# A hybrid attention block on one core: the first attention block prepared during the last weight tile, and group B's last product packed into one bank

## The reference

```python
proj = x @ W_in                       # one projection, its columns shared out
# group A: 8 query heads, one key/value head
dots  = qi . ki                       # 4 index heads
score = sum_h w_h * relu(dots)        # per query and key, chunk-causal
idx   = top_k(score, 256)             # per query
ya    = softmax(qa . ka[idx] / 8 - slope * |distance|) @ va[idx]
# group B: 8 query heads, 2 key/value heads, window of 128 keys, a sink per head
yb    = softmax([qb . kb / 8 - slope * |distance|, sink])[:-1] @ vb
y     = concat(ya * silu(ga), yb * silu(gb)) @ W_out
out   = layer_norm(2 ** 0.25 * x + y) * g + b
```

## Time and profile before

| | before |
|---|---|
| median of 3 runs | 1454.12 us (1453.76 to 1454.82) |
| profiled execution | 1462.23 us, span 1460.4 us |
| PE busy | 1359.3 us (93%) |
| DVE busy | 1130.6 us (77%) |
| ACT busy | 896.8 us (61%) |
| POOL busy | 629.6 us (43%) |
| last product ends, first scan starts | 555.7 us, 572.1 us |
| output projection starts | 1275.8 us |

### The profile page before, as it was taken

The page is one execution under the profiler, slowest core; times in us unless marked ns, Lnnn a source line. Parts: engine busy times, 40 slices in busy tenths (PEclk is TensorE's granted clock), DMA queues, the critical chain, the costliest instruction groups (busy, mean ns, idle before and its releaser), DMA issues. The chain is left out here.

```text
span 1460.4 us, 18810 instructions
## 1 busy us (share of the span) xinstructions
PE 1359.3 (93%) x6006; PEld 993.5 (68%) x6052; DVE 1130.6 (77%) x2215; ACT 896.8 (61%) x1687; POOL 629.6 (43%) x726
## 2 busy tenths in 40 slices
PE   7999999899999995798999799999999799999997
PEld 5888887698888874565655456655555565588886
DVE  3486879864899887778889999889898967257675
ACT  3395885873498736777775488885678676700010
POOL 2421332633422336466544256534336577423332
PEclk9999999999999996699999999999999899999999
DMA  7412232325232328233433132402011143134442
GB/s 241 127 60 80 87 105 80 117 91 154 73 109 94 101 90 174 66 89 87 113 92 88 45 83 56 104 21 64 27 28 26 39 133 118 44 122 146 144 148 83
DMA packets 106548, 136.85 MB, mean 94 GB/s; under 512 B 6643, under 2 KB 83383, under 8 KB 106191
## 3 DMA queue, kind: packets, MB, share of 16 engines
q1 hardware_dynamic: 93296, 93.23, 23.4%
q10 hardware_dynamic: 9504, 31.66, 5.5%
q0 software_dynamic: 3648, 10.76, 2.5%
HBM read 92.20 MB, written 42.34 MB: 92 GB/s over the span
## 5 line engine op out<-in xcount | busy, mean ns | idle before, releaser
L1644 DVE TENSOR_SCALAR_CACHE_REDUCE above<-dist,trial 128x512 bf16<-128x512 int32 (+13 forms) x224 | 345.9, 1544 | 28.9 <-POOL trial L1002 23.9
L1179 ACT ACTIVATE above<-dist,trial 128x384 bf16<-128x384 int32 (+13 forms) x224 | 280.8, 1254 | 60.8 <-DVE trial L1617 24.3
L1356 PE MATMUL psum<-x_hi,w_hi 128*128 128x512 f32 x640 | 251.8, 393 | 16.0 <-DVE x_lo L1693 10.6
L1356 PE MATMUL psum<-x_lo,w_hi 128*128 128x512 f32 x640 | 250.8, 392 | 0.0
L1356 PE MATMUL psum<-x_hi,w_lo 128*128 128x512 f32 x640 | 250.5, 391 | 0.0
L1290 ACT ACTIVATE prob<-psum 128x512 f32<-128x512 f32 x272 | 159.8, 593 | 115.8 <-PE psum L1506 54.6
L1748 DVE CUSTOM_DVE_ANT_0 junk<-psum,mask 128x512 bf16<-128x512 f32 (+3 forms) x320 | 184.4, 605 | 26.7 <-PE psum L1430 16.1
L1506 PE MATMUL psum<-prob,vw 128*65 128x512 f32 x376 | 184.8, 597 | 0.1
L1493 PE MATMUL psum<-qa_mix,ka_mix 128*128 128x512 f32 x272 | 162.4, 597 | 5.5 <-DMA qa_ext<-minus_max 3.7
L1430 PE MATMUL psum<-ka_ext,qa_ext 128*128 128x512 f32 (+3 forms) x320 | 134.1, 467 | 27.4 <-ACT ka_mix L1129 12.3
L941 POOL CAST w_hi<-raw 128x1024 fp32r<-128x1024 f32 x40 | 49.7, 1243 | 253.1 <-PE psum L1356 248.8
(11 more groups left out here) (161 smaller groups left out, 2906.8 us busy)
## 6 DMA issues: line engine op xcount, KB each, us to landing
raw<-w_tiles SPq DMA_DIRECT2D x40, 512.0 KB, 3.7
proj<-staged ACTq DMA_DIRECT2D x40, 512.0 KB, 3.3
qb_raw<-proj SPq DMA_DIRECT2D x32, 256.0 KB, 4.0
qa_raw<-proj SPq DMA_DIRECT2D x32, 256.0 KB, 4.5
yt_raw<-y_t SPq DMA_DIRECT2D x16, 512.0 KB, 5.1
x_row<-x_res SPq DMA_DIRECT2D x16, 512.0 KB, 3.9
out<-z ACTq DMA_DIRECT2D x16, 512.0 KB, 2.6
x_raw<-xT SPq DMA_DIRECT2D x12, 512.0 KB, 4.2
```

What stands on the lines that cost most here:

```text
L1179: nc.scalar.activation(above[:, 0, 0:n], src, ACT.Sign, scale=-1.0, bias=u, accum_out=count[:, 0:1]).then_inc(sign_counted, 1)
L1356: last = pe.matmul(psum[:, 2 * u + m, :], wt[:, u, k, :], xt[:, k, 512 * m:512 * m + 512], start=(k == 0 and q == 0), stop=(k == KT - 1 an ...
L1644: v.tensor_scalar(above[:, 1, 0:n], src, u, None, ALU.is_ge, ALU.add, accum_out=count[:, 1:2]).then_inc(own_counted, 1)
```

## The change

Three things are edited, and a fourth follows from them.

1. **Earlier conditions at the seam.** The products of the last tile now count up `x_used` for each k slice. `last_tile(k)` waits for one slice instead of the whole tile, and the loads, POOL's DMAs and the first rounding of queries use slices 0 to 6 by what each overwrites; three late tensors are placed elsewhere for that (`qa_raw`, `junk` and `y_a`). Group A's keys are read into `values_hi` and `values_lo` instead of `relu`, during the second half of the projection, and are rounded there; `split_values` waits for them. The first scan waits for the evacuation of the last tile but one.
2. **Constants on POOL.** The memsets of `setup_pieces` move from DVE to POOL (`fill`), each behind the slice that frees its place.
3. **Group B's last product.** Each of the four matmuls of `mix_b` has 64 weight columns, writes 64 rows, and all go to bank 2; `gate_b` is one instruction of 128 rows in place of two of 64.
4. **A new order.** All 165 numbers of `PREFER` differ, and POOL's decisions cost 0.53 instead of 0.45 in the plan, so nearly every engine's order differs from the first microseconds on.

```diff
-PREFER = {'above': -36689.1, 'band0': -163507.6, 'band1': 5353.3,
+PREFER = {'above': -229823.5, 'band0': -129160.3, 'band1': -191364.3,
...
-    add("SP", 0.7, "load_keys_a", needs=[sums[-1], ("store", 1, 2)])
+    last = lambda k: ("product", 1, N_TILES - 1, k)
+    add("SP", 1.4, "load_keys_a", needs=[("store", 1, 2)])
...
-    add("DVE", 1.8, "setup_dve", needs=[end])
+    for i in range(2):
+        add("POOL", 0.35 if i else 2.2, "fill", i, needs=[end if i else last(5), ("fill", i - 1)])
...
-        keys_a_raw = flat(relu)
+        keys_a_raw = [values_hi[:, :, :].bitcast(F32).rearrange("p b n -> p (b n)")[:, 0:HALF],
+                      values_lo[:, :, :].bitcast(F32).rearrange("p b n -> p (b n)")]
+
+        def last_tile(k):
+
+            return (x_used, KT + k) if k < KT - 1 else (tile_mm, 2 * N_TILES)
...
             def load_keys_a():
                 sp.wait_ge(stored[0], 16 * (N_TILES // 2 + 2))
-                sp.wait_ge(summed, 4 * chunks_before(NPAIR - 2))
...
             def extra_rows():
-                pool.wait_ge(tile_mm, 2 * N_TILES)
+                pool.wait_ge(*last_tile(4))
...
+            def fill(top):
+
+                pieces = [(2, mask[:, 0, 0:P], 0.0), (2, mask[:, 1, 0:2 * P], 0.0), (2, mask[0:HD, 0, HD:P], -BIG),
+                          (2, mask[0:HD, 1, P + HD:2 * P], -BIG), (2, lb[:, :, 0:HD], 0.0), (5, vs[0:HD, 0, :], 0.0),
+                          (KT - 1, row_top[:, :], 0.0)]
...
             def round_keys_a(i):
                 ks = slice(HALF * i, HALF * (i + 1))
-                act.wait_ge(keys_in, 32)
+                act.wait_ge(keys_in, 64)
+                act.wait_ge(x_lo_ok, 2 * KT + 2)
...
-                    pe.wait_ge(tile_out, 2 * N_TILES)
+                    pe.wait_ge(tile_out, 2 * N_TILES - 1)
...
+                        rows = slice(HD * g, HD * g + HD)
-                        last = pe.matmul(psum[:, 2 + g, 2 * P * c:2 * P * c + 2 * P], keys, ptb[:, g, 2 * P * c:2 * P * c + 2 * P],
+                        last = pe.matmul(psum[rows, 2, 2 * P * c:2 * P * c + 2 * P], keys[:, rows], ptb[:, g, 2 * P * c:2 * P * c + 2 * P],
                                          start=True, stop=True)
...
-                for g in range(2):
-                    rows = slice(HD * g, HD * g + HD)
-                    last = v.tensor_tensor(yt_b[rows, :, :].rearrange("p h (c q) -> p c h q", c=2),
-                                           psum[rows, 2 + g, :].rearrange("p (c h q) -> p c h q", c=2, h=4),
-                                           gate_b[rows, :, :].rearrange("p h (c q) -> p c h q", c=2), ALU.mult)
-                last.then_inc(b_gated, 1)
+                v.tensor_tensor(yt_b[:, :, :].rearrange("p h (c q) -> p c h q", c=2),
+                                psum[:, 2, :].rearrange("p (c h q) -> p c h q", c=2, h=4),
+                                gate_b[:, :, :].rearrange("p h (c q) -> p c h q", c=2), ALU.mult).then_inc(b_gated, 1)
```

More of the change, by code:

```diff
@@ L215, in dots_of @@
                 add("DVE", 0.33 + n / 960, "search", p, i, needs=[start, ("decide_own", p, i - 1)])
-                add("POOL", 0.45, "decide_own", p, i, needs=[("search", p, i)])
+                add("POOL", 0.53, "decide_own", p, i, needs=[("search", p, i)])
                 add("ACT", 0.49 + (n - P) * 0.00083, "sign", p, i, needs=[start, ("decide_sign", p, i - 1)])
-                add("POOL", 0.45, "decide_sign", p, i, needs=[("sign", p, i)])
+                add("POOL", 0.53, "decide_sign", p, i, needs=[("sign", p, i)])
             else:
@@ L337, in whole_plan @@
         add("POOL", 3.6, "split_qb", b, needs=[("round_qb", b)])
-        add("SP", 0.7, "load_qa", b, needs=[("split_qa", b - 1)] + ([end] if first else []))
+        add("SP", 0.7, "load_qa", b, needs=[("split_qa", b - 1)] + ([last(0), ("store", 1, 7)] if first else []))
         if b >= 2:
             add("SP", 0.4, "load_mask", b, needs=[("store_masks", b // 2), last_values(b - 2)])
-        add("ACT", 1.75, "round_qa", b, needs=[("load_qa", b)] + ([last_values(b - 2)] if b >= 2 else [end]))
+        add("ACT", 1.75, "round_qa", b, needs=[("load_qa", b)] + ([last_values(b - 2)] if b >= 2 else [last(KT - 2)]))
         add("POOL", 2.0 if b else 0.9, "positions", b, needs=[("extra_rows",)] + ([last_values(b - 2)] if b >= 2 else []))
@@ L348, in whole_plan @@
             add("DVE", 1.45, "bias_b", b, g,
-                needs=[("window", b, g), ("turn_b", b - 1), ("load_bias",), ("setup_dve",), ("put_sink", b), ("exp_b", b - 1, H - 1)])
+                needs=[("window", b, g), ("turn_b", b - 1), ("load_bias",), ("fill", 0), ("put_sink", b), ("exp_b", b - 1, H - 1)])
         for h in range(H):
@@ L360, in whole_plan @@
                 needs=[("round_qa", b), ("positions", b), ("leave_max", b - 1), scan_list[-2], ("scan", *scan_list[-1][1:]),
-                       ("extra_rows",), ("load_power",), ("round_keys_a", 1), ("evacuate", 1, N_TILES - 1)])
+                       ("extra_rows",), ("load_power",), ("round_keys_a", 1), ("evacuate", 1, N_TILES - 2)])
             scan_list.append(("scan_max", *scan))
-            add("DVE", 0.16 + w * 0.00104, "scan_max", *scan, needs=[("scan", *scan), ("load_mask", b), ("setup_dve",), scan_list[-2], *stores])
+            add("DVE", 0.16 + w * 0.00104, "scan_max", *scan, needs=[("scan", *scan), ("load_mask", b), ("fill", 1), scan_list[-2], stores[1], end])
         if b >= 4:
@@ L372, in whole_plan @@
         add("PE", 1.8, "mix_b", b, needs=[("copy_b", b), ("shift_values",)], holds="banks2", until=("gate_b", b))
-        add("DVE", 1.35, "gate_b", b, needs=[("mix_b", b), ("load_gate_b", b), ("store_b", b - 1)])
+        add("DVE", 0.71, "gate_b", b, needs=[("mix_b", b), ("load_gate_b", b), ("store_b", b - 1)])
         add("POOL", 1.0, "store_b", b, needs=[("gate_b", b)])
@@ L1359, in product @@
                     last.then_inc(tile_mm, 1)
[L1360 removed]
+                elif t == N_TILES - 1:
                     last.then_inc(x_used, 1)
@@ L1741, in scan_max @@
                 if scan == 0:
-                    for i in range(2):
-                        dve.wait_ge(stored[i], 16 * N_TILES)
+                    dve.wait_ge(stored[0], 16 * N_TILES)
+                    dve.wait_ge(tile_mm, 2 * N_TILES)
+                    dve.wait_ge(filled, FILLS)
                 dve.wait_ge(a_scan, scan + 1)
```

85 lines of the change are left out of this document (40 added, 45 removed).

## The result

The changed kernel takes 1461.0 us (median of 4 runs, 1459.35 to 1462.96) against 1453.94 for the kernel before in the same measurement: ratio 1.0049, interval 1.0032 to 1.0067. It is 0.5% slower, about 7 us. Its profiled execution took 1460.82 us, span 1459.0. The time lies inside the predicted range of 1430 to 1462, near its top, but the sign is wrong: the forecast was 1445. The range held it because it had been drawn over the rivals too; alone the forecast spanned 1437 to 1451.

The account below looks back on a forecast made before the run. PE and DVE were taken to bound the kernel in turns, with DVE's chain of pairs behind. Seam +5.5, start +2, gates -6.9 and pair 6 -9 gave -8.4 us: 1445 us forecast, chance 0.36, range 1430 to 1462.

Parts of the forecast that it names:

- The seam's PE side: End of projection: products end 9.1 us earlier, first scan 6 to 8 us behind; 9 to 12 us gained for PE alone.
- The lateness of pair 4: Second projection half: ten dots pieces later, so pair 5's first sum comes 13.6 us later, at 539.3.
- 15 us idle for the same work: DVE from pair 5's first sum to block 1's leave_max: 15 us idle instead of about 20, winning 5 back.
- +5.5: DVE's chain at the seam, at block 1's leave_max: 13.6 - 5 - 1.1 - 2, so 5.5 us later.
- Pair 6, -9: Around 825 us: PE's waits for y_a and block 8's leave_max go, 9 us gained, bounds 0 and 13.
- The rest of the order, 0 with 6 either way: Pieces moved throughout the kernel: no row gives a sign, so 0 with 6 us either way.
- Gates -6.9: gate_b as one instruction saves DVE 0.69 us in ten blocks where DVE leads: -6.9 us, bounds 0 and 11.
- PE's term 0: mix_b on PE: same columns and place in the chain, so no change; bounds 3.5 us either way.
- That rival: mix_b: the two key groups' matmuls run side by side, about 6 us more gained, 1439 us; chance 0.03.
- The start, +2: First projection half: PE waits 2 us for low parts before norm pieces; bounds +1.5 and +3.6.
- the late pairs decide: Sums of pair 4: the 13.6 us pass whole, y_a's stall returns; +5.6 us, 1460 us; chance 0.26.
- the forecast's own signs of being wrong: Pair 5's first sum not late, block 1's leave_max well before 600, or PE idling over 10 us up to pair 6's sortable end.

Follow-up runs that it names:

- e0: The kernel before, unchanged, run again for a second profile; 1455.93 us.
- e2: The changed kernel with group B's product as before (128 weight columns, two banks, two gate instructions), in the new order; ratio 1.0121 to the kernel before.
- e1: The kernel before with only group B's product changed, every engine's order untouched; 1451.34 us, ratio 0.9974.
- e7: e1 with the last scans and leave_max of block 8 ahead of pair 6's sortable, and scans and logits ahead of block 7's columns_a; 1457.68 us.
- e3: All edits of the changed kernel, PE's and DVE's order as in the kernel before, group A's keys rounded earlier, ahead of a relu; 1456.78 us.
- e4: The changed kernel with the order of the kernel before from the first search step of pair 6 on; 1461.5 us, ratio 1.0036.
- e5: e3 with group A's keys rounded during sortable of pair 4, so all edits in the old order; 1443.47 us, ratio 0.9915 to the kernel before.
- e9: The changed kernel's new order up to the last product, from there the order of the kernel before; 1455.28 us, ratio 1.0010.
- e12: e5 with all pieces of pair 4, dots, relu and sums of pair 5, and the keys' copies 13.7 us later; 1462.53 us.
- e15: e5 without block 0's early conditions: of the seam only the keys stay early; 1450.3 us, ratio 0.9962 to the kernel before.
- e10: e5 with only dots, relu and sums of pairs 4 and 5 (and the keys' copies behind them) 13.7 us later; 1468.32 us, ratio 1.0105.
- e11: As e10 with half the delay, 6.85 us; 1462.1 us, ratio 1.0056 to the kernel before.
- e13: All edits; new order only up to the end of tile 1 of the second half, then the order of the kernel before; 1455.77 us.
- e16: All edits; new order only up to the last product of the first half, then the order of the kernel before; 1452.63 us.
- e6: The changed kernel with mix_b packed into one bank but gate_b as two instructions of 64 rows; 1470.37 us, ratio 1.0095.
- e14: e1 with both key groups' matmuls writing rows 0 to 63, group 1's into bank 3; ratio 1.0005 to the kernel before.
- e17: The changed kernel with the order of the kernel before up to the last product of the first half; 1462.41 us, ratio 1.0044.

## Why the prediction was wrong, step by step

**The seam's PE side** held: the last product ended at 545.3 and the first scan started at 550.1 (said: about 549, and 6 to 8 us behind; it was 4.8), and the wait for the keys is gone.

**The lateness of pair 4** held too: 13.6 us were predicted at the first sum of pair 5 (539.3; the 541 in the list of signs does not follow from the sum), and 13.0 were measured against e0.

**"I give the changed kernel 15 us idle for the same work"** is the step that failed first. The term was +5.5 (bounds -4.5 and +10.5), read at `leave_max` of block 1. DVE's chain does not pass there any more. Measured with group B's change taken out (e2 against e0), the kernel is 13.3 us late at Q6 (841.9 against 828.6), where seam and pair 6 together had -3.5. Busy time from S5 to Q6 (the third pair of numbers is DVE), e0 first, then e2:

```profile
526.00:828.56 302.56, 253.44 (x1087) 168.51 (x1104) 255.89 (x591) 208.91 (x383) 149.03 (x215) 0.91 0.41 98
539.60:841.85 302.25, 257.20 (x1098) 167.32 (x1113) 266.51 (x617) 208.30 (x398) 145.63 (x223) 0.90 0.39 95
```

Over this longer stretch DVE's idle time fell from 46.7 to 35.7 us, more than the 5 I gave. What failed is "for the same work": DVE's busy time there rose by 10.6 us, where I had taken 3.1 off, and so nothing of the lateness came back. Of the 10.6 us, 8.0 are the second line of the sums, which got slower (below; 25.3 us in e2 from 520 to 600, 17.4 in e0), and the rest is not split here; three gate instructions more stand ahead of Q6. In the changed kernel the sums of pair 5 took 46.0 us (539.0 to 585.0) instead of 29.6, with scans and biases between them.

**Pair 6, -9,** failed outright: "What follows, 850 to 1100, is PE-bound, with 25.9 us free on DVE, so the gain stays." The wait for `y_a` went, but from the first sum of pair 6 to Q6 it is 51.7 us in the changed kernel and 51.6 in e0 and e1; in the old order a smaller form of the edit costs 5 us (e7). A full PE from 850 on was no proof that PE would make up for a late Q6. With group B's edit and the old order of the late part, the time from Q6 to OP is 437.1 to 437.2 us in seven kernels (e1, e3, e4, e5, e9, e12, e15) and 436.2 to 438.5 in the other four (e10, e11, e13, e16), while Q6 moves from 819.9 to 843.1. So what DVE's chain is late at Q6 reaches the end nearly undiminished. This doesn't make DVE the limit behind Q6: from e0 to e1 PE's busy time in that leg falls by 5.1 us and the leg by 3.9, so PE's work counts there. It is the start of the leg that the chain of pairs sets.

**The rest of the order, 0 with 6 either way:** with group B undone the leg from Q6 to OP is 447.5 instead of 441.0, +6.5, just past the bound; with it done, +1.5.

**Group B.** Gates -6.9: measured -6.7 in this order (e6; by the table 3.1 of it from S5 to Q6 and 4.0 behind it, where I had counted nothing for 850 to 1100), but nothing visible up to Q6 in the old one. That the number came out is luck in part: it had the gain in other blocks. PE's term 0: measured up to -3.8 in the old order (e1, all of its gain) and about as much in the new one, not clear of noise. "The order speaks against it" was wrong. I had argued that both products of group 0 are issued first, so only one pair could meet; the trace shows all four meeting in two pairs. The row on which I leaned had matmuls with 65 and 64 columns that write rows from 0 on, and so could not show what different rows do. That rival's mechanism was true, with a chance of 0.03. The Trainium skill says that tiles run independently (TensorEngine Tiling (Array Packing), Tiling Modes), and the traces of e1 and e14 agree, with PE's busy time in `mix_b` at 19.2 us in e1 and 34.0 in e14. It also names a drain for a change of mode, which I had ruled out by the 0.22 us between two products of the earlier trace rows. At `mix_b` something of that sign does show: the gap of 0.52 us behind it in e14 against 0.25 before. It is smaller than what side by side running saves, and that it is the drain was not tried by itself.

**The start, +2:** PE waited 1.5 us for `wn_lo`. It is part of the 13.0 at S5 at most; e17 without it is as slow.

**The sum.** I had -1.5 without group B and -6.9 with it. Measured by ratio it is +17.6 (e2) and -10.5. The rival "the late pairs decide" (+5.6, 1460 us) had the mechanism and the place: the pairs more than 12 us late, and the pairs behind win none back (S5 to Q6 is 302.3 in e2 and 302.6 in e0). That it had nearly the time as well is luck: without group B it had +12.5 against +17.6 measured, with group B -6.9 against -10.5, and the two errors nearly cancel. Two of the forecast's own signs of being wrong came, `leave_max` of block 1 at 578.4 and PE idle for 10.6 of the 80 us up to the end of pair 6's `sortable`.

## What to carry to other kernels

Find the chain whose lateness arrives at the end undiminished, by marks that every variant passes, before pricing anything by an engine's share of busy time; an engine that is full in a late stretch may only be full of work that another chain released. When an edit comes with a new order, run the edit in the old order first: here that is 0.85% faster than before, and the new order turned it into 0.5% slower. And look behind a wait before paying for its removal: another of the same length may stand there.

## What was unexpected of the hardware

A sum on DVE gets slow beside POOL. Timeline of DVE in the changed kernel: three equal instructions, the first beside nothing on POOL but the issue of a DMA.

```profile
539.51 0.75 DVE L1613 SCALAR_TENSOR_TENSOR score<-relu,vw,score 128x512 f32<-128x512 f32 x1
...
561.75 1.65 DVE L1613 SCALAR_TENSOR_TENSOR score<-relu,vw,score 128x512 f32<-128x512 f32 x1
...
566.79 2.27 DVE L1613 SCALAR_TENSOR_TENSOR score<-relu,vw,score 128x512 f32<-128x512 f32 x1
```

POOL in the same time:

```profile
561.37 3.16 POOL L1043 TENSOR_TENSOR qb_mix<-qb_raw,qb_mix 64x512 fp32r<-64x512 f32 x2
566.48 2.03 POOL L1052 TENSOR_TENSOR lb<-lb,rec_b 128x1024 f32<-128x1024 f32 x1 [1.95 <-DVE rec_b L1777]
```

The second and third took 0.9 and 1.5 us longer, each beside a POOL instruction. From 520 to 600 the 24 instructions of this line are busy 25.7 us in the changed kernel and 17.4 in e0 (17.4 in e5): 8.3 us on the very chain that counts, in an order that puts the sums beside block 0's preparation on POOL. The Trainium skill has this rule (SBUF — State Buffer, Who interferes with whom): a DVE instruction with two SBUF inputs contends with a GpSimd instruction that reads SBUF. These rows agree; I didn't try it by itself.
